# Expert weight chunks of 2 contraction tiles by 1024 columns in place of 4 by 512

## The reference

```python
aff = jax.nn.softmax((h @ w_router).astype(jnp.float32), axis=-1)
gates, idx = lax.top_k(aff.transpose(0, 2, 1), cap)
def one(hb, gb, ib):
    xe = hb[ib]
    hid = jax.nn.silu(jnp.einsum('ecd,edf->ecf', xe, w_gate)) * jnp.einsum('ecd,edf->ecf', xe, w_up)
    ye = jnp.einsum('ecf,efd->ecd', hid, w_down) * gb[..., None].astype(hb.dtype)
    return jnp.zeros_like(hb).at[ib.reshape(-1)].add(ye.reshape(-1, D))
```

## Time and profile before

| | |
|---|---|
| median of 3 runs | 1945.41 us (1941.34 to 1945.91) |
| the profiled execution: its own time, and its span | 1945.45 us, 1943.6 us |
| PE busy | 1822.5 us (94%) |
| DVE busy | 1487.4 us (77%) |
| ACT busy | 1155.3 us (59%) |
| read from HBM | 488.50 MB |

### The profile page before, as it was taken

One profiled execution on the slowest core, in us unless ns is written; L12 is line 12 of the kernel. 1 busy time (PEld: TensorE's weight loads), 2 busy tenths in 40 slices (PEclk: granted clock), 3 DMA queues, 4 the chain that ended last, 5 costly groups with the idle time before them and its releaser, 6 DMA issues.

```text
span 1943.6 us, 24164 instructions
## 1 busy us (share of the span) xinstructions
PE 1822.5 (94%) x8673; PEld 1290.0 (66%) x8673; DVE 1487.4 (77%) x1419; ACT 1155.3 (59%) x1185; POOL 393.8 (20%) x209
## 2 busy tenths in 40 slices
PE   4899999999888879579999999999999999999996
PEld 2688677877777768446666666666666666666664
DVE  4589545533377766779989989998998999899895
ACT  5444333232367761257777777777777777777773
POOL 0255401100011110003023213302321330232121
PEclk8899999999889999689999999999999999999998
DMA  8333543353222222389999999999999999999993
GB/s 284 129 119 134 196 162 126 119 169 128 83 76 66 76 66 98 115 282 373 382 376 379 384 383 379 380 382 379 378 381 381 378 382 380 379 376 383 382 380 118
DMA packets 273666, 511.35 MB, mean 263 GB/s; under 512 B 12348, under 2 KB 38244, under 8 KB 273608
## 3 DMA queue, kind: packets, MB, share of 16 engines
q1 hardware_dynamic: 264808, 487.48, 69.5%
q0 software_dynamic: 8800, 23.09, 4.2%
HBM read 488.50 MB, written 22.04 MB: 263 GB/s over the span
## 4 chain that ended last, share of the span: by engine, by line
PE 82%; DVE 6%; POOL 4%; DMA 2%; ACT 2%; SPq 2%; issue 1%; DVEq 0%; ACTq 0%; POOLq 0%
PE banks L1435 25%; PE banks L1436 24%; PE banks L1437 24%; POOL qk_swp L1331 2%; PE banks L1597 2%; POOL qk_swp L1326 1%; DMA v_h<-v_scr 1%; PE banks L1454 1%; PE banks L1455 1%; DVE w_lo L883 1%; PE banks L1693 1%; PE banks L1569 1%; PE banks L1660 1%; DVE nbias L1110 1%; DVE qk_raw L977 1%
## 5 line engine op out<-in xcount | busy, mean ns | idle before, releaser
L1295 DVE TENSOR_TENSOR w_lo<-raw_x,w_hi 128x2048 fp32r<-128x2048 f32 x192 | 437.5, 2286 | 65.4 <-ACT w_hi L861 63.7
L1295 DVE TENSOR_TENSOR w_lo<-raw,w_hi 128x2048 fp32r<-128x2048 f32 x189 | 430.9, 2287 | 35.0 <-ACT w_hi L861 31.4
L861 ACT ACTIVATE w_hi<-raw 128x2048 fp32r<-128x2048 f32 x189 | 362.7, 1919 | 110.7 <-PE banks L1437 109.2
L861 ACT ACTIVATE w_hi<-raw_x 128x2048 fp32r<-128x2048 f32 x192 | 368.0, 1917 | 84.8 <-PE banks L1437 83.8
L1435 PE MATMUL banks<-w_hi,xe_hi 128*80 128x512 f32 x1024 | 405.9, 396 | 2.2 <-issue 2.2
L1436 PE MATMUL banks<-w_hi,xe_lo 128*80 128x512 f32 x1024 | 403.8, 394 | 0.0
L1437 PE MATMUL banks<-w_lo,xe_hi 128*80 128x512 f32 x1024 | 400.1, 391 | 0.0
L1411 POOL DMA_INDIRECT out<-yeg,idx_l x32 | 146.8, 4586 | 831.5 <-DVE yeg L1257 831.5
L1435 PE MATMUL banks<-w_hi,h_hi 128*128 128x512 f32 x560 | 223.4, 399 | 2.0 <-POOL h_lo L1318 1.0
L1436 PE MATMUL banks<-w_hi,h_lo 128*128 128x512 f32 x560 | 221.7, 396 | 0.0
L1437 PE MATMUL banks<-w_lo,h_hi 128*128 128x512 f32 x560 | 221.2, 395 | 0.0
(11 more groups left out here) (200 smaller groups left out, 2230.7 us busy)
## 6 DMA issues: line engine op xcount, KB each, us to landing
raw<-in_w_gate_e SPq DMA_DIRECT2D x80, 1024.0 KB, 6.7
raw_x<-in_w_down_e SPq DMA_DIRECT2D x80, 1024.0 KB, 7.0
raw<-in_w_up_e SPq DMA_DIRECT2D x64, 1024.0 KB, 6.4
raw_x<-in_w_up_e SPq DMA_DIRECT2D x64, 1024.0 KB, 6.7
raw_x<-in_w_gate_e SPq DMA_DIRECT2D x48, 1024.0 KB, 6.0
raw<-in_w_down_e SPq DMA_DIRECT2D x48, 1024.0 KB, 6.9
raw<-in_w_in SPq DMA_DIRECT2D x28, 1024.0 KB, 5.6
raw<-in_w_ada SPq DMA_DIRECT2D x24, 1024.0 KB, 6.2
```

Of the source, the lines that this page charges most:

```text
L861: nc.scalar.activation(w_hi[:, j % NSPLIT], raw_slot(slot), ACT.Copy).then_inc(hi_done, 1)
L1295: nc.vector.tensor_tensor(w_lo[:, j % NSPLIT], raw_slot(EXPERT_SLOT[j % NRAWE]), w_hi[:, j % NSPLIT], ALU.subtract).then_inc(lo_done, 1)
```

## The change

A chunk is now 2 contraction tiles by 1024 columns, still 1 MB. Its rows in HBM are 4 KB long and not 2 KB, so a load has 256 rows and not 512. Chunks 0 to 3 are `w_gate` for the first 1024 hidden columns, 4 to 7 `w_up` for them, 8 to 11 and 12 to 15 the same for the other 1024; chunks 16 to 23 are `w_down`, each with all 1024 output columns. So two banks are filled at a time: 0 and 2 by gate, 1 and 3 by up, 4 and 5 by down. The number of matmuls, their shapes and the number of chunks stay. The tables put the small steps of two blocks one step apart, and both output halves are multiplied by `gate2` at step 0 of the next expert (after the loop for the last). Lengthy parts are cut:

```diff
-SG_STEP = {4 * fb + 2: fb for fb in range(4)}
-HID_STEP = {4 * fb + 4: fb for fb in range(4)}
-HT_STEP = {4 * fb + 5: fb for fb in range(4)}
-HTO_STEP = {4 * fb + 6: fb for fb in range(4)}
-YE_STEP = 20
+SG_STEP = {8 * (fb // 2) + 4 + fb % 2: fb for fb in range(4)}
+HID_STEP = {8 * (fb // 2) + 8 + fb % 2: fb for fb in range(4)}
+HT_STEP = {8 * (fb // 2) + 9 + fb % 2: fb for fb in range(4)}
+HTO_STEP = {8 * (fb // 2) + 10 + fb % 2: fb for fb in range(4)}
...
+            w, k, c = (w_gate, w_up)[i // 4 % 2], i % 4 * 2, i // 8 * 2 * CW
+        else:
+            w, k, c = w_down, (i - 16) * 2, 0
+        if isinstance(e, int):
+            return w[e, :, k:k + 2, c:c + 2 * CW]
...
+    def wide(slot):
+
+        return slot.rearrange("p (k c) n -> p k (c n)", c=2)
...
-                        act.wait_ge(chunk_read, e * EC + i)
+                        act.wait_ge(chunk_read, e * EC + 8 * (fb // 2) + 4)
...
-                dve.wait_ge(chunk_read, e * EC + (YE_STEP + 4 * half))
+                dve.wait_ge(chunk_read, e * EC + EC)
...
-                        dve.wait_ge(chunk_read, e * EC + 4 * (fb + 1))
+                        dve.wait_ge(chunk_read, e * EC + 8 * (fb // 2 + 1))
...
+                        hf, which, q = i // 8, i // 4 % 2, i % 4
+                        ps = [bank(2 * c + which)[0:CAP, :] for c in range(2)]
+                        if q == 0 and not (first and hf == 0):
+                            pe.wait_ge(hid_ready if which else sg_ready, e * 4 + 2 * hf)
...
+                        q = i - 16
+                        ps = [bank(4 + c)[0:CAP, :] for c in range(2)]
                         if q == 0 and not first:
+                            pe.wait_ge(yeg_ready, e * 2)
+                        if q % 2 == 0:
+                            pe.wait_ge(ht_ready, e * 4 + (q // 2 + 1))
...
+                    for k in range(2):
+                        if k == 1 and i in HT_STEP:
+                            hid_transposes(e, HT_STEP[i])
+                        kk = 2 * q + k
+                        c = slice(kk * CAP, (kk + 1) * CAP)
+                        for half in range(2):
+                            last = split3(ps[half], st[0][:, c], st[1][:, c], w_hi[:, s, 2 * k + half, :], w_lo[:, s, 2 * k + half, :],
+                                          kk == 0, kk == kt - 1)
```

More of the change, by code:

```diff
@@ L299, in expert_source @@
         if i < 16:
[L300 to L305, removed]
+            w, k, c = (w_gate, w_up)[i // 4 % 2], i % 4 * 2, i // 8 * 2 * CW
[3 more added lines that the diff above has]
+            return w[e, :, k:k + 2, c:c + 2 * CW]
+        return w[bass.ds(e, 1), :, k:k + 2, c:c + 2 * CW].rearrange("e p k n -> p (e k) n")
     base = (nc.sbuf_base + 31) // 32 * 32
@@ L532, in load @@
                     sp.wait_ge(lo_done, n - NRAW + 1)
-                src = chunk_source(n) if n < PRE else expert_source(0, n - PRE)
-                sp.dma_start(raw[:, n % NRAW], src).then_inc(raw_in[n % NRAW], 16)
+                dst, src = (raw[:, n % NRAW], chunk_source(n)) if n < PRE else (wide(raw[:, n % NRAW]), expert_source(0, n - PRE))
+                sp.dma_start(dst, src).then_inc(raw_in[n % NRAW], 16)
             for i, name in enumerate(["c", "c_ctx", "norm1_g", "norm2_g"]):
@@ L619, in _ @@
             for i in range(NRAW, NRAWE):
-                sp.dma_start(raw_slot(i), expert_source(0, i)).then_inc(raw_in[i], 16)
+                sp.dma_start(wide(raw_slot(i)), expert_source(0, i)).then_inc(raw_in[i], 16)
             sp.dma_start(gate2[0:CAP_L, :], gate_d[0, 1:2, :].broadcast_to([CAP_L, D])).then_inc(gate2_in, 16)
@@ L634, in expert_loads @@
                     sp.wait_ge(lo_done, e * EC + (PRE + i + 1))
-                    sp.dma_start(raw_slot(slot), src).then_inc(raw_in[slot], 16)
+                    sp.dma_start(wide(raw_slot(slot)), src).then_inc(raw_in[slot], 16)
             expert_loads(0, False)
@@ L1269, in expert @@
                     if i == 0 and not first:
-                        gated_output(e - 1, 1, isinstance(e, int) and e == 1)
+                        if isinstance(e, int) and e == 1:
+                            dve.wait_ge(gate2_in, 32)
+                        for half in range(2):
+                            gated_output(e - 1, half, isinstance(e, int) and e == 1)
                     fb = HID_STEP.get(i)
@@ L1284, in expert @@
                                                 hT_hi[:, 4 * fb:4 * fb + 4, :], ALU.subtract).then_inc(ht_ready, 1)
[L1285 to L1288, removed]
                     if i in XM_STEP and not last:
@@ L1302, in _ @@
             expert(E - 1, False, True)
-            gated_output(E - 1, 1, False)
+            for half in range(2):
+                gated_output(E - 1, half, False)
         @block.gpsimd
@@ L1701, in expert @@
                     if i < 16:
[L1702 to L1712, removed]
-                    else:
-                        half, q = (i - 16) // 4, (i - 16) % 4
-                        ps = bank(4 + half)[0:CAP, :]
+                        hf, which, q = i // 8, i // 4 % 2, i % 4
@@ L1716, in expert @@
+                        ps = [bank(2 * c + which)[0:CAP, :] for c in range(2)]
+                        if q == 0 and not (first and hf == 0):
+                            pe.wait_ge(hid_ready if which else sg_ready, e * 4 + 2 * hf)
+                        st, kt = (xe_hi, xe_lo), KT
+                    else:
+                        q = i - 16
+                        ps = [bank(4 + c)[0:CAP, :] for c in range(2)]
                         if q == 0 and not first:
-                            pe.wait_ge(yeg_ready, e * 2 + (half - 1))
@@ new lines, in expert @@
+                        st, kt = (hT_hi[:, :, :].rearrange("p f c -> p (f c)"), hT_lo[:, :, :].rearrange("p f c -> p (f c)")), FE // P
+                    for k in range(2):
[3 more added lines that the diff above has]
+                        c = slice(kk * CAP, (kk + 1) * CAP)
+                        for half in range(2):
+                            last = split3(ps[half], st[0][:, c], st[1][:, c], w_hi[:, s, 2 * k + half, :], w_lo[:, s, 2 * k + half, :],
+                                          kk == 0, kk == kt - 1)
```

## The result

The changed kernel took 1966.45 us (median of 6 runs, 1963.33 to 1969.24), the kernel before 1943.55 us on the same occasions (6 runs, 1940.69 to 1948.74). The ratio is 1.0119, with a 95% interval of 1.0104 to 1.0133: 22.9 us slower. The profiled execution took 1966.2 us, its span is 1964.4 us, 20.8 more than before.

A forecast was written before the change was run, and what follows sets the result against it. TensorE (PE) alone was taken to set the time, with DVE about 10% from the limit. New wait 22.7 us plus end 3.35 us gave 26.0 on 1945.45: 1971.5 us, range 1963 to 1986, at 72%.

The forecast's parts named there:

- The new wait: Second block's transposes on PE wait for bank 6, emptied by DVE's `hT_lo`: 0.84 or 0.56 us each, 22.7 us in all.
- DVE's five starts: DVE's row `hid`, `w_lo`, `hid`, `w_lo`, `hT_lo` after the last up chunk; `hT_lo` starts at 7.58 us, ends at 8.06.
- The release: From the end of DVE's `hT_lo` to the start of PE's waiting transposes: 0.06 us.
- the restart: After PE's wait ends, the next matmul starts 0.35 us later and not 0.23: 0.12 us added per wait.
- Matmuls: PE's expert matmuls, changing bank after every third: pace unchanged, taken as 0, with 15.4 us bounding a pace difference.
- The end: After the last expert's last matmul, a second pair of scatters adds 3.35 us, or 5.15 if its first is slow.
- Loads: Expert weight loads with half as many rows of twice the length: hidden, 0 us; landing sooner, with a lower transfer share.
- The other small steps: Moved SiLU, output products, token steps and scatters in the expert loop stay hidden: 0 us.
- Hidden wait: Rival: DVE reaches `hid` early enough that `hT_lo` is in time, only the end's cost remains: 1948.8 us; 8%.
- freed matmuls: Rival: transfers slow TensorE in the expert loop and longer rows free it, gaining 15.4 us: 1933.4 us; 4%.
- a DVE that falls behind: Rival: DVE falls behind at steps 16 to 22, up to 2 us more per expert: 2004 us; 9%.
- that danger: Rival: PE's waits in the expert loop lower TensorE's clock, 1.5 us after each, 48 us added: 2019.5 us; 7%.

The follow-up runs named there:

- experiment 1: Changed kernel with the second block's transposes of each pair two chunks behind the first's, not one: 1947.16 us, ratio 1.0015 to the kernel before.
- experiment 3: Changed kernel with every 1 MB expert load issued as two of 512 KB with 2 KB rows: 1966.90 us, ratio 1.0118 to the kernel before.
- experiment 5: Changed kernel with DVE's `hT_lo` of blocks 0 and 2 moved behind the next `w_lo`, enlarging PE's wait: 2117.54 us, ratio 1.0904.
- experiment 4: Kernel before with only both output halves' gate2 products moved to step 0 of the next expert, and after the last: 1947.71 us, ratio 1.0022.

## Why the prediction was right, point by point

- *The number.* 26.0 us more were forecast and 22.9 measured (20.2 to 25.8 by the interval of the ratio). The time itself was forecast at 1971.5 us and is 1966.45: 3.1 us of the distance are this difference, and 1.9 that the kernel before took 1943.55 us on these occasions and not 1945.45.
- *Bound.* TensorE alone set the time: each of its pauses showed in full, and no change to loads or to ACT's slack did.
- *The new wait.* From the last matmul of chunk 7, DVE's five starts were forecast at 1.84, 2.50, 4.71, 5.37 and 7.58 us; the timeline has 1.81, 2.48, 4.68, 5.34 and 7.54. The release took 0.14 (1214.95 to 1215.09) and not 0.06, and of the 0.12 for the restart 0.03 showed: the first matmul behind the transposes starts 0.27 us after them (1215.09 to 1215.36) and not 0.24, as behind those at 1211.29 (to 1211.53). Two small terms were wrong, and it was luck that they cancel, 0.17 us together against 0.18. By difference between the changed kernel and experiment 1, the pause costs 0.81 us in the first pair and 0.51 in the second, forecast 0.84 and 0.56. The sum was forecast at 22.7 us and is 21.65.
- *Matmuls.* I took 0, out of bounds of 0 and 15.4 us. They gained: 2.753 us for a chunk against 2.760, 2.3 us in all (1084.01 to 1081.73 us for the loop, in the kernel before and in experiment 1). This is the larger of the two errors. With the wait's 1.0 it makes 3.3 us, and loop and end in the two traces together are indeed 22.7 us longer.
- *The end.* 3.35 us forecast, 3.3 measured, with and without the rest of the change.
- *Loads.* Nothing gained or lost, as forecast, and experiment 3 shows it. But I said that they would land sooner, and they did not. The share did fall.
- *The other small steps* were forecast at 0, and the experts' other chunks kept their length but for that change of pace, so they were hidden.
- *The marks to look for.* I gave 3.6 us for chunk 18, and it took 3.83. That was a slip: the token transposes stand in this chunk too, so that my own terms give 2.76 + 0.28 + 0.28 + 0.56 = 3.88. The sum is not touched. The expert was forecast at 69.3 us and took 69.13.
- *Rivals.* Hidden wait, freed matmuls and a DVE that falls behind did not come. The Trainium skill, TensorE: Matmul & The Clock Gate, A second HAM failure mode, warns of short idle times between groups of matmuls that write to changing banks. At 0.8 and 0.5 us of idle time, once each in 69 us, the trace shows a clock of 1.00 throughout the loop, so that danger does not reach this far. At 3.5 us (experiment 5) the clock did fall.

## What to carry to other kernels

When small steps are brought together so that two larger tiles can be filled at a time, look for the single buffer that both pass through, here one PSUM bank, and write down the row order of the engine that empties it: the pause was five starts added up, and each was right to 0.04 us. The pause is removed by distance on the waiting engine; moving the emptying ahead on the engine that does it also helped, but it gave a quarter of it back in other waits. A transfer that nobody waits for gives nothing when it becomes more efficient, however full its engines are.

## What the runs showed of the hardware

- Two pauses, of 0.8 and 0.5 us, in every 69 us left TensorE's granted clock at 1.00; pauses of 3.5 us at the same places brought it to 0.50 again and again. That cost some 54 us in the loop, beside the 95.5 us by which the waits grew.
- Matmuls of 512 columns came 0.2295 us apart with banks changed every three, and 0.2300 with a bank kept for six or for a whole chunk. The order of the left operands made no difference. Why the chunks alternate between 2.73 and 2.77 us with the change is left open.
- Rows of 4 KB in place of 2 KB took the transfers' share from 1.05 to 0.99 at nearly the same rate, and loads landed no sooner. The moved output products are the likely reason, since their two pairs of scatters now come together: in experiment 4, which moved them and kept rows of 2 KB, loads landed in 6.1 to 8.1 us, as late as with the change (6.2 to 8.1), against 6.0 to 7.0 before. These are medians of one trace each; an effect of the row length on the landing does not show in them.
